# Ten weight products: the first weight piece of each copied, split and waited for in four quarters

## The reference, cut to what matters

```
p = u @ w_in                                   # first block; even_mixer and odd_mixer of the second block
m = o @ w_out                                  # the same three
f = (silu(u @ w_gate) * (u @ w_up)) @ w_down   # four feed-forward layers
```

## Time and profile before

| | us |
|---|---|
| median of 3 runs | 3709.95 |
| lowest and highest | 3709.57 and 3710.76 |
| time of the profiled execution | 3707.65 |
| its span, from first to last instruction | 3705.8 |
| its mean granted TensorE clock | 0.918 of 2.4 GHz |

### The profile page before, as it was taken

The page is one execution under the profiler, slowest core; times in us unless marked ns, Lnnn a source line. Parts: engine busy times, 40 slices in busy tenths (PEclk is TensorE's granted clock), DMA queues, the critical chain, the costliest instruction groups (busy, mean ns, idle before and its releaser), DMA issues. The chain is left out here.

```text
span 3705.8 us, 43953 instructions
## 1 busy us (share of the span) xinstructions
PE 3125.1 (84%) x17862; PEld 2422.8 (65%) x17862; DVE 1317.9 (36%) x1626; ACT 1016.5 (27%) x1332; POOL 213.9 (6%) x180
## 2 busy tenths in 40 slices
PE   4996765877758999897877999899989868679999
PEld 0994562323226888776766888688879645578887
DVE  3226742111114332344444331433233546433322
ACT  2114520000013221334223221322133435422222
POOL 0001000000000000100101000100010007210000
PEclk8997977999978999897888999899989989889999
DMA  8213148999973332220013332333222200213332
GB/s 327 80 50 138 38 173 334 427 427 427 428 297 89 91 101 93 78 83 1 2 62 87 102 92 101 80 95 97 99 72 91 70 12 1 69 57 102 95 98 85
DMA packets 299330, 486.30 MB, mean 131 GB/s; under 512 B 15297, under 2 KB 259484, under 8 KB 283838
## 3 DMA queue, kind: packets, MB, share of 16 engines
q1 hardware_dynamic: 294394, 466.82, 35.8%
q10 hardware_dynamic: 2500, 9.23, 0.6%
q0 software_dynamic: 2304, 8.39, 0.6%
HBM read 457.13 MB, written 27.28 MB: 131 GB/s over the span
## 5 line engine op out<-in xcount | busy, mean ns | idle before, releaser
L393 PE MATMUL psum_banks<-u_high,f_ffn_w_high 128*128 128x512 f32 x1408 | 551.8, 392 | 31.1 <-DVE f_ffn_w_low L2501 31.1
L394 PE MATMUL psum_banks<-u_low,f_ffn_w_high 128*128 128x512 f32 x1408 | 550.7, 391 | 0.0
L395 PE MATMUL psum_banks<-u_high,f_ffn_w_low 128*128 128x512 f32 x1408 | 550.6, 391 | 0.0
L2501 DVE TENSOR_TENSOR f_ffn_w_low<-weight_pieces,f_ffn_w_high 128x2048 fp32r<-128x2048 f32 x132 | 302.2, 2292 | 407.2 <-ACT f_ffn_w_high L2466 407.2
L2466 ACT ACTIVATE f_ffn_w_high<-weight_pieces 128x2048 fp32r<-128x2048 f32 x132 | 251.3, 1906 | 331.8 <-PE psum_banks L395 322.1
L393 PEld LDWEIGHTS psum_banks<-u_high,f_ffn_w_high 128*128 128x128 f32 x1408 | 266.4, 189 | 88.4 <-DVE f_ffn_w_low L2501 32.7
L394 PEld LDWEIGHTS psum_banks<-u_low,f_ffn_w_high 128*128 128x128 f32 x1408 | 266.5, 189 | 55.1
L395 PEld LDWEIGHTS psum_banks<-u_high,f_ffn_w_low 128*128 128x128 f32 x1408 | 266.1, 189 | 55.5
L1825 PE MATMUL psum_banks<-expert_ring,experts_x_t 128*64 128x512 f32 x1024 | 243.9, 633 | 39.7 <-DMA expert_ring<-in_expert_w_up 38.3
L393 PE MATMUL psum_banks<-f_ffn_w_high,f_hidden_high 128*128 128x512 f32 x704 | 274.2, 390 | 3.6 <-issue 3.6
L395 PE MATMUL psum_banks<-f_ffn_w_high,f_hidden_low 128*128 128x512 f32 x704 | 273.9, 389 | 0.0
(11 more groups left out here) (625 smaller groups left out, 5412.9 us busy)
## 6 DMA issues: line engine op xcount, KB each, us to landing
expert_ring<-in_expert_w_gate SPq DMA_DIRECT2D x32, 2048.0 KB, 35.2
expert_ring<-in_expert_w_up SPq DMA_DIRECT2D x32, 2048.0 KB, 36.3
expert_ring<-in_expert_w_down SPq DMA_DIRECT2D x32, 2048.0 KB, 40.4
weight_pieces<-in_ffn_w_gate SPq DMA_DIRECT2D x88, 512.0 KB, 4.0
weight_pieces<-in_ffn_w_up SPq DMA_DIRECT2D x88, 512.0 KB, 5.3
weight_pieces<-in_ffn_w_down SPq DMA_DIRECT2D x88, 512.0 KB, 4.1
entry_w<-in_w_ada SPq DMA_DIRECT2D x24, 1024.0 KB, 18.3
weight_pieces<-in_odd_w_in SPq DMA_DIRECT2D x20, 1024.0 KB, 5.3
```

Source lines behind the costliest of these rows:

```text
L393: nc.tensor.matmul(out, lhs.high, rhs.high, start=start, stop=False, skip_group_check=True)
L394: nc.tensor.matmul(out, lhs.high, rhs.low, start=False, stop=False, skip_group_check=True)
L395: return nc.tensor.matmul(out, lhs.low, rhs.high, start=False, stop=stop, skip_group_check=True)
L2501: nc.vector.tensor_tensor(w.low[:, j], raw[:, j], w.high[:, j].bitcast(F32), ALU.subtract).then_inc(w_low, 1)
```

## The change

The activation and the subtraction of the first chunk or piece of each of the ten blocks are cut in four along the columns (in `project` along the k tiles: two of eight each, four of sixteen in `odd_out`). Each quarter has a semaphore step of its own: the first three count `first_high` and `first_low`, the last one counts `high_ok` and `low_ok` (`w_high`, `w_low` in the feed-forward), so later counts stay as they were. PE waits for a quarter just ahead of the first matmul that reads it. To have such waits at the first chunk alone, the first pair of chunks is written out ahead of PE's loop, which starts at the second pair. Code of ACT, DVE and SP loops is unchanged.

```
+FIRST = 4
...
+        first_high, first_low = s.sem("first_high"), s.sem("first_low")
+        per_first = k_tiles // FIRST
...
-                with pe.Fori(0, part.pairs) as i:
-                    for j in range(2):
-                        c = i * 2 + j
-                        pe.wait_ge(low_ok, c + (part.chunks + 1))
+
+                def products(c, j):
+                        first = part is walk[0] and isinstance(c, int) and c == 0
+                        if not first:
+                            pe.wait_ge(low_ok, c + (part.chunks + 1))
...
                             for q in range(k_tiles):
+                                if first and u == 0 and q % per_first == 0:
+                                    if q // per_first < FIRST - 1:
+                                        pe.wait_ge(first_low, q // per_first + 1)
+                                    else:
+                                        pe.wait_ge(low_ok, 1)
...
+                alone = 1 if part is walk[0] else 0
+                if alone:
+                    products(0, 0)
+                    products(1, 1)
+                if part.pairs > alone:
+                    with pe.Fori(alone, part.pairs) as i:
+                        for j in range(2):
+                            products(i * 2 + j, j)
...
+                if slot_free is None:
+                    for n in range(FIRST):
+                        qs = slice(n * per_first, (n + 1) * per_first)
+                        nc.scalar.activation(w.high[:, j, qs], raw[:, qs], ACT.Copy).then_inc(first_high if n < FIRST - 1 else high_ok, 1)
+                    return
...
+            def low(c, j, slot_free):
+                if slot_free is None:
+                    for n in range(FIRST):
+                        qs = slice(n * per_first, (n + 1) * per_first)
+                        if n < FIRST - 1:
+                            v.wait_ge(first_high, n + 1)
+                        else:
+                            v.wait_ge(high_ok, 1)
+                        nc.vector.tensor_tensor(w.low[:, j, qs], raw[:, qs], w.high[:, j, qs].bitcast(F32),
+                                                ALU.subtract).then_inc(first_low if n < FIRST - 1 else low_ok, 1)
+                    return
```

`ffn_products` gets the same three edits, with `per_first` = 512 columns (four of the sixteen 128 by 128 tiles, so the first two quarters are the gate half) and PE's loop from the second pair on:

```
+            products(0, 0)
+            products(1, 1)
+            with pe.Fori(1, pairs) as i:
+                for j in range(2):
+                    products(i * 2 + j, j)
...
-            high(0, None)
+            for n in range(FIRST):
+                cols = slice(n * per_first, (n + 1) * per_first)
+                nc.scalar.activation(w.high[:, 0, cols], raw[:, 0, cols], ACT.Copy).then_inc(first_high if n < FIRST - 1 else w_high, 1)
             high(1, None)
```

More of the change, by code:

```diff
@@ L2375, in ffn_products @@
         down_mm, tile_mm, ahead_in = s.sem("down_mm"), s.sem("tile_mm"), s.sem("ahead_in")
+        first_high, first_low, per_first = s.sem("first_high"), s.sem("first_low"), 2 * KD * P // FIRST
         post, junk, stats = s.sb("post_gain", [P, D]), s.sb("junk", [P, D]), s.sb("stats", [P, 2 * NT + 1])
@@ L2423, in _, with products @@
             pe.sem_inc(up_mm, 1)
[L2424 to L2427, removed]
+            def products(t, j):
+                    first = isinstance(t, int) and t == 0
+                    if not first:
+                        pe.wait_ge(w_low, t + 1)
                     pe.wait_ge(whole_ok, t + 1)
@@ L2431, in _ @@
                             at = (side * KD + q) * P
+                            if first and at % per_first == 0:
+                                if at // per_first < FIRST - 1:
+                                    pe.wait_ge(first_low, at // per_first + 1)
+                                else:
+                                    pe.wait_ge(w_low, 1)
                             last = product(nc, k.ps[:, 2 * j + side, :], w[:, j, at:at + P], u[:, q, :], q == 0, q == KD - 1)
                         last.then_inc(sem, 1)
+            products(0, 0)
[3 more added lines that the diff above has]
+                    products(i * 2 + j, j)
             def down(b, j, first=False, final=False):
@@ L2511, in _ @@
             v.sem_inc(whole_ok, 2)
-            low(0, 0)
+            for n in range(FIRST):
+                cols = slice(n * per_first, (n + 1) * per_first)
+                if n < FIRST - 1:
+                    v.wait_ge(first_high, n + 1)
+                else:
+                    v.wait_ge(w_high, 1)
+                nc.vector.tensor_tensor(w.low[:, 0, cols], raw[:, 0, cols], w.high[:, 0, cols].bitcast(F32),
+                                        ALU.subtract).then_inc(first_low if n < FIRST - 1 else w_low, 1)
             with v.Fori(0, pairs) as i:
```

1 line of the change is left out of this document (removed).

## The result

The changed kernel took 3688.99 us in the median of five runs (3688.18 to 3699.69). The kernel before took 3709.95 us beside it. The ratio is 0.9944, with a 95% interval of 0.9929 to 0.9958, so the change saves 21 us, between 16 and 26. The forecast was 3678.2 us, 31.8 us less. The time lies inside the range of 3673 to 3691, but a third of the expected gain is missing.

What follows compares the result with a forecast made beforehand. PE, busy 84% of the span, was taken to wait at each start for a high and a low copy in a row. 26.0 + 5.8 = 31.8 us less than 3709.95 gave 3678.2 us, range 3673 to 3691.

Steps and rivals of the forecast that it cites:

- nothing else holds PE there: At the start of `f0`: PE waits 4.28 us only for a chain of one activation and one subtraction.
- The chain at the start, nine blocks: Starts of nine blocks: first matmul 1.39 us after ACT's start, not 4.28; 2.89 us earlier each, 26.0 us.
- Extra work on ACT and DVE: Quartered pieces: 0.6 and 0.5 us more busy time a block, beside PE's matmuls; zero cost.
- second-chunk rival: Mixer products: PE waits for the second chunk, so they gain only 5 x 1.1 + 2.4 us; 3690.6 us, chance 0.07.
- the later quarters: After each start: quarters follow every 0.60 us (1.13 in `odd_out`), faster than PE uses them; no wait, zero.
- the second chunk: Six mixer products: PE still finds the chunk ready, least room in `even_qkvz`, 0.9 us left of 2.6; zero, but thin.
- the branch: Loop entry between second and third chunk in nine blocks: no gap seen in the profile, taken as zero.
- Below zero it cannot be: Mid-stream loop entry in nine blocks: its cost can't be negative, since a branch saves nothing.
- The rival of 3720.5 us: Loop entries in nine blocks: PE runs out of fetched code and waits 4.7 us each, 42.3 us; chance 0.03.
- The clock: Ten starts at half clock, 40.84 us together: the rise moves with the start, nothing gained or lost on average.
- The rival by which it stays put: Ten starts: clock rises at the same moment as before, half of 31.8 us is left; 3694.1 us, chance 0.04.
- the statement that would prove me wrong: One of three signs, on the ten starts: the slow stretches together are far from 41 us.

Runs made afterwards that it cites:

- hoist: Changed kernel with the credit for the PSUM banks given ahead of the first split; 3684.36 us, ratio 0.993, and 3683.97 us, ratio 0.9926, once more.
- peel_only: Kernel before with only PE's first pair written out ahead of the loop in all ten blocks, nothing cut in quarters; 3711.1 us, ratio 0.9998.
- after_copy: The changed kernel unedited, measured for the third time; 3692.33 us, ratio 0.9947 to the kernel before.
- hoist8: Changed kernel with the bank credit ahead of the first split and the first piece cut in eight, not four; 3678.01 us, ratio 0.991.
- ffn_only: Quarters in the four feed-forward blocks alone, the six mixer products as in the kernel before; 3695.4 us, ratio 0.9964.
- mixers_only: The six mixer products as in hoist, the four feed-forwards as in the kernel before; 3692.02 us, ratio 0.9952.
- before_copy: The kernel before, unedited, measured and profiled once more; 3712.1 us in eleven runs, ratio 1.0.
- high_first: As hoist8, but in `f0` to `f3` and `even_qkvz` the first two matmuls wait for the high copy alone; 3678.11 us, ratio 0.9903.

## Why the prediction was right, and where it was wrong

**Right: what bounds the starts.** PE waited at each start for a chain of two instructions and nothing else in the feed-forward. The chain got shorter as read: 1.50 us in place of 4.28, 2.78 us less, where the forecast had 2.89. The first pieces took 0.63 and 0.69 us as taken from the earlier trace rows; the handovers from ACT to DVE to PE together take about 0.2 us and not 0.07. That is 0.11 us in each feed-forward. Over all ten blocks, with the credit out of the way as in hoist, the starts give 31.1 us where 31.8 were booked: a small error of 0.7.

**Wrong: "nothing else holds PE there".** This was read in `f0` and carried over to all nine blocks of the step "The chain at the start, nine blocks", and to `odd_out`. In the six mixer products a second thing was hidden under the first: the bank credit, which stands behind the split in DVE's queue and goes out when ACT's whole high copy is done. Before the change that was 1.96 us behind ACT's start (3.66 in `odd_out`), over 2 us ahead of the low copy, and the waits named only the low copy. With the change it is 2.23 us (3.94), later than the first low quarter. Starts were 2.31 and 4.02 us in place of 1.50 and 2.46: 5.6 us, shown by hoist, which moves the credit and nothing else. The clue stood in two places ahead of time. PE's row of the first matmul lists two waits, for the first quarter and for `proj_out_bank_free_v`; and the trace of before has the credit at 1.96 us, which is no way to a start at 1.39. The step "Extra work on ACT and DVE" asked what is queued behind the quarters, and named only the second piece of the feed-forward. A saving of 2.89 us was booked where 1.98 to 2.06 came, and 5.8 where 4.18 came.

**That the time lies in the range was luck.** The range reached up to 3691 for the sake of the second-chunk rival. The forecast's own worst case, all clock starts as long as the longest, ends at 3687.9, and the measured 3689.0 lies above it.

**Right: the later quarters, the second chunk, the branch.** No wait of PE for a later piece, with four or with eight. No wait for the second chunk in any profile, also not in hoist, where PE comes 0.8 us earlier than in the changed kernel. The forecast saw the least room in `even_qkvz`; in hoist it is in `odd_in`, 0.77 us. The rule of the Trainium skill on taken branches, in "Runtime: NRT & Kernel Launch", section "Instruction fetch mechanics", does not cost anything here: 0.12 us at the entry, and ratio 0.9998 with the written-out pair alone. No run shows whether a target lay outside the fetched window, so the rule itself is not tested. "Below zero it cannot be" was slightly wrong: with the entry behind them, four starts come 0.08 us earlier (peel_only). The rival of 3720.5 us is refuted, and that of 3690.6, though it nearly gives the measured time, is refuted too. It needed waits at the second chunk, and there are none.

**The clock: mechanism kept, the size read from one profile was chance.** All ten starts are slow in every profile, as forecast; `f0` of the changed kernel is so after 4.12 us of idleness. Their sum is 49.8, about 44 and 46 us in three profiles of the changed kernel, and 40.8 and 47.1 in two of the kernel before. So the rise moves with the start, give or take. The rival by which it stays put would have made them longer by the whole gain of the starts, 25 us together. They grew by 9, 3 and 5 us against the one profile of before, and by 3, -3 and -1 against the other. The rule cited from the Trainium skill, "TensorE: Matmul & The Clock Gate", section "What's actually happening" (the windows run freely), fits: the slow stretch of the first start, `mix_in`, took from 2.8 to 6.1 us in twelve profiles. What the profiles show is this scatter; what makes it they don't. But the statement that would prove me wrong, ten stretches far from 41 us, was badly set, since one execution of the unchanged kernel is 6 us off by itself.

**The account of single executions.** From the starts alone the changed kernel gains 4 x 2.79 + 2 x 1.98 + 3 x 2.06 + 4.18 = 25.5 us. Between the profiles of before and after the span fell by 7.9 us only. The starts give -25.5, the clock +4.5, the slow pitch +8.7 (384 + 768 + 768 matmuls in `proj_out`, `odd_in` and `odd_out`, 4.5 ns each), the time up to `mix_in` +1.0, and the stage from `proj_out` to `f0` another 3.6, in all -7.7. For after_copy, without slow pitch, it is -25.5 + 2.7 + 0.9 + 2.0 = -19.9, against 3685.9 - 3705.8 = -19.9 measured.

**What stays open.** By medians the changed kernel gained 21, 20 and 20 us in three comparisons, where the starts count 25.5. The missing 5 us lie inside each interval, but not in the three together: the mean of its 15 runs lies 20.6 us below that of the 36 runs of before, with a standard error of 1.1. Hoist and hoist8 fall short by 3 to 5 as well, while ffn_only and mixers_only do not on the sum. Two candidates are the clock and the pitch. In the four profiles whose mixer products start as before (before, before_copy, peel_only, ffn_only) 2 of 20 blocks were slow, 1.3 us a profile; in the eight others 13 of 40, 4.8 us a profile. The slow stretches sum to some 43 us in the four and 46 in the eight, of which half counts. Together that is about the missing 5 us, but single profiles scatter by more, and the link isn't shown. A third candidate is the stage between `proj_out` and `f0`, 656.6 to 663.3 us long over twelve profiles, with no order by program. For some 400 us of it the DMA engines are full, here in the profile of after:

```profile
700.00:800.00 100.00, 78.89 (x326) 29.24 (x324) 11.21 (x12) 1.79 (x3) 0.00 (x0) 0.86 1.01 427
```

A stage that streams the experts' weights at 427 GB/s can give back what PE won at the two starts ahead of it. No run separated this; it isn't shown.

## What to carry to other kernels

When one instruction is cut into pieces so that a consumer can start early, list every semaphore that the consumer's first instruction waits for, and find where each increment stands in its producer's queue. One that stood behind the single instruction now stands behind the last piece, and behind that piece's wait. The view of the waits names only the one that ended last. A second one that ended over 2 us earlier didn't show in it, but its increment has a row of its own, by source line: its time is the earliest start that a shorter first wait can give, and it can be read before anything is changed. And before a profile is used to account for a few us in 3700, take the profile of the unchanged kernel twice. Here the second one moved by 6 us.

With the credit ahead of the split and eight pieces (hoist8, 3678.0 us, ratio 0.991) the kernel beats both versions, by 33 us and by about 13 (33.4 - 20.8, each from its ratio); with the high copy first (high_first, 3678.1, ratio 0.9903) it is as fast within the measurement.

## What the hardware showed that was not expected

The same matmul of 256 columns, at full granted clock and with no idle time, follows the one ahead after 113.3 ns in some blocks and after 117.8 ns in others, for the whole block. Which blocks are slow differs between executions of one program, also of the unedited kernel (`odd_out` in before_copy). In twelve profiles there were 0 to 3 slow blocks of the five, worth 1.7 to 5.2 us each (384 to 1152 matmuls, 4.5 ns each). Only the last part of `mix_in`, 192 matmuls, was slow in every profile. The 512-column matmuls of the feed-forward showed 226.7 ns in all twelve. What chooses between the two was not found.
